# Sparse attention in a three-layer kernel: compression weights in long rows, requested at the last group's products, and one bias table of 256 columns a head

## What is computed

```python
def compress(kv, pos, w1, w2):
    idx = jnp.arange(n_cmp)[:, None] * CMP_STRIDE + jnp.arange(CMP_BLOCK)[None, :]   # 15 blocks of 32, stride 16
    blocks = kv[:, idx] + pos[None, None, :, None, :]
    flat = blocks.transpose(0, 1, 3, 2, 4).reshape(B, n_cmp, G, CMP_BLOCK * D)
    return jax.nn.silu(flat @ w1) @ w2                                               # w1: 4096 x 128
...
    kc = compress(k_cmp, cmp_pos_k, cmp_k_w1, cmp_k_w2)
    vc = compress(v_cmp, cmp_pos_v, cmp_v_w1, cmp_v_w2)
    bias_c = table[rel_bucket(dist_c)]
    logits_c = jnp.einsum('bsghd,bigd->bghsi', qf, kc) + bias_c
    p_c = masked_softmax(logits_c, mask_c, -1)
    o_c = jnp.einsum('bghsi,bigd->bsghd', p_c, vc)
...
    o = gt[:, :, 0] * o_c + gt[:, :, 1] * o_s + gt[:, :, 2] * o_w                    # compressed, selected, window
```

## Time and profile before

| | |
|---|---|
| median of three runs | 1650.07 us (1648.35 to 1650.73) |
| profiled execution | 1647.93 us |
| its span in the trace | 1646.1 us |
| TensorE busy | 1600.4 us, 97% |
| VectorE, ScalarE, GpSimd busy | 990.7 us (60%), 792.4 us (48%), 93.1 us (6%) |
| mean granted clock of TensorE | 0.994 of full |
| DMA | 253.85 MB, mean 154 GB/s |

### The profile page before, as it was taken

The page is one execution under the profiler, slowest core; times in us unless marked ns, Lnnn a source line. Parts: engine busy times, 40 slices in busy tenths (PEclk is TensorE's granted clock), DMA queues, the critical chain, the costliest instruction groups (busy, mean ns, idle before and its releaser), DMA issues. The chain is left out here.

```text
span 1646.1 us, 32613 instructions
## 1 busy us (share of the span) xinstructions
PE 1600.4 (97%) x14261; PEld 1539.4 (94%) x14261; DVE 990.7 (60%) x1320; ACT 792.4 (48%) x1128; POOL 93.1 (6%) x83
## 2 busy tenths in 40 slices
PE   8999999999998999989999999999999999999999
PEld 7989998899997899989999899999998999999999
DVE  6686547756354664485545688887557654455643
ACT  6643226333333854454443488775455334444432
POOL 2120004000000001040000000000010000000000
PEclk9999999999998999999999999999999999999999
DMA  9543323433285337548676444444654645555572
GB/s 293 187 129 104 91 91 103 154 91 91 80 226 147 93 101 257 179 101 230 188 199 182 142 142 141 142 145 144 217 157 148 206 143 165 143 165 181 169 215 90
DMA packets 80021, 253.85 MB, mean 154 GB/s; under 512 B 9153, under 2 KB 18402, under 8 KB 79624
## 3 DMA queue, kind: packets, MB, share of 16 engines
q1 hardware_dynamic: 79224, 251.57, 50.7%
q0 software_dynamic: 656, 0.21, 0.1%
HBM read 249.06 MB, written 2.69 MB: 153 GB/s over the span
## 5 line engine op out<-in xcount | busy, mean ns | idle before, releaser
L307 DVE TENSOR_TENSOR w_lo<-w_raw,w_hi 128x1024 fp32r<-128x1024 f32 (+1 forms) x452 | 549.5, 1220 | 482.5 <-ACT w_hi L302 481.9
L302 ACT ACTIVATE w_hi<-w_raw 128x1024 fp32r<-128x1024 f32 (+1 forms) x452 | 470.5, 1045 | 575.9 <-PE ps L360 460.8
L358 PE MATMUL ps<-xt,w_hi 128*128 128x256 f32 x2224 | 652.8, 294 | 11.5 <-DVE w_lo L307 7.9
L359 PE MATMUL ps<-xt,w_hi 128*128 128x256 f32 x2224 | 632.7, 284 | 0.0
L360 PE MATMUL ps<-xt,w_lo 128*128 128x256 f32 x2224 | 632.1, 284 | 0.0
L358 PEld LDWEIGHTS ps<-xt,w_hi 128*128 128x128 f32 x2224 | 429.7, 193 | 31.0 <-issue 19.5
L359 PEld LDWEIGHTS ps<-xt,w_hi 128*128 128x128 f32 x2224 | 430.2, 193 | 1.5 <-issue 1.0
L360 PEld LDWEIGHTS ps<-xt,w_lo 128*128 128x128 f32 x2224 | 429.8, 193 | 0.0
L368 PE MATMUL ps<-w_hi,xt 128*128 128x256 f32 x576 | 169.3, 294 | 0.0
L369 PE MATMUL ps<-w_lo,xt 128*128 128x256 f32 x576 | 162.8, 283 | 0.0
L370 PE MATMUL ps<-w_hi,xt 128*128 128x256 f32 x576 | 162.8, 283 | 0.0
(11 more groups left out here) (401 smaller groups left out, 1756.8 us busy)
## 6 DMA issues: line engine op xcount, KB each, us to landing
w_raw<-in_a_w_in SPq DMA_DIRECT2D x128, 512.0 KB, 3.6
w_raw<-in_w_in SPq DMA_DIRECT2D x120, 512.0 KB, 3.6
w_raw<-in_b_w_in SPq DMA_DIRECT2D x96, 512.0 KB, 3.6
w_raw<-in_w_out SPq DMA_DIRECT2D x32, 512.0 KB, 3.6
w_raw<-in_a_w_out SPq DMA_DIRECT2D x32, 512.0 KB, 3.7
w_raw<-in_b_w_out SPq DMA_DIRECT2D x32, 512.0 KB, 3.9
arena<-in_x SPq DMA_DIRECT2D x4, 512.0 KB, 6.6
w_raw<-in_w_in SPq DMA_DIRECT2D x8, 256.0 KB, 4.3
```

Source lines behind the costliest of these rows:

```text
L302: k.nc.scalar.activation(k.wh[:, p % RING, 0:m], k.raw[:, p % RAW, 0:m], ACT.Copy).then_inc(k.hi_made, 1)
L307: k.nc.vector.tensor_tensor(k.wl[:, p % RING, 0:m], k.raw[:, p % RAW, 0:m], k.wh[:, p % RING, 0:m].bitcast(F32), ALU.subtract).then_inc(k. ...
L358: pe.matmul(os, h[:, cs], xh, start=st and ct == 0, stop=False, skip_group_check=True)
L359: pe.matmul(os, h[:, cs], xl, start=False, stop=False, skip_group_check=True)
```

## The change

`cmp_k_w1` and `cmp_v_w1` are arranged on the host into one input `cmp_w1` of 128 x 2 x 32 x 128 numbers, so that a partition's numbers lie in one row. The weights are requested in five transfers of 0.5, 1, 1, 1 and 0.5 MB. The first four (all but steps 8 to 15 of the keys' weights, whose room the recurrent mixer still uses) wait for the last products of the last group (`mm_`), with a piece behind each; then come two of the bias transfers, and after `half_done` the fifth, the second weights and the other six bias transfers.

The bias table of a head is one window of 256 columns, and the first tile reads its second half; all 8 heads stand in one room of the arena, filled by 8 transfers of 16 partitions, where 32 were. `before(h)` makes two additions (256 and 512 numbers) where one of 768 was, and `pre` counts both. The copies into `cbias` are 2 where 4 were. `NSA_WAIT` is 36 where 60 was: all stages of the sparse mixer from the second on stand 24 slots earlier (the compression at 799, the last at 963). A small scratch tile of the recurrent mixer (`small`) moves out of the arena into the room of `state`.

```diff
-NSA_A, NSA_WAIT = 5, 60
+NSA_WAIT = 36
...
+        self.bias = ar[:, 8192:8192 + NSA_H * S].rearrange("p (h n) -> p h n", h=NSA_H)
...
-    def loads(self, sp, g, done):
+    def loads(self, sp, g, products, last, done):
...
         k, a = self.k, self.a
+        w1 = a["cmp_w1"]
+        g.load(sp, products)
+        for par in range(2):
+            sp.wait_ge(last[par], 2 * sum(G_PE))
+        for i, (n, ls) in enumerate(((0, slice(0, 8)), (0, slice(16, 32)), (1, slice(0, 16)), (1, slice(16, 32)))):
+            sp.dma_start(self.w1[:, n, ls], w1[:, n, ls]).then_inc(k.w1_in, 16)
+            g.load(sp, products + 1 + i)
+        sp.wait_ge(k.rows_out, 32)
+        parts = skewed_parts(k, sp, self.bias, 0, NSA_H, self.bi)
+        for c in range(2):
+            next(parts)
         g.load(sp, done)
         sp.wait_ge(k.half_done, 2)
-        for n, nm in enumerate(("cmp_k_w1", "cmp_v_w1")):
-            sp.dma_start(self.w1[:, n], a[nm][0].rearrange("(l d) o -> d l o", d=P)).then_inc(k.w1_in, 16)
-            g.load(sp, done + 2 + 2 * n)
+        sp.dma_start(self.w1[:, 0, 8:16], w1[:, 0, 8:16]).then_inc(k.w1_in, 16)
...
-            g.load(sp, done + 5 + c // 2)
+        for c in range(2, P // SKEW):
+            next(parts)
+            g.load(sp, done + c // 2)
...
-                pe.wait_ge(self.pre, h)
+                pe.wait_ge(self.pre, 2 * h)
...
-        pe.wait_ge(k.w1_in, 32)
+        pe.wait_ge(k.w1_in, 80)
...
-            nc.vector.scalar_tensor_tensor(out=self.sc[:, h % 3], in0=k.ps[:, 0:2, 0:3 * P], scalar=scale,
-                                           in1=view(self.table(h)[:, 0:1], [[0, 2], [1, 3 * P]]),
-                                           op0=ALU.mult, op1=ALU.add).then_inc(self.pre, 1)
-            dve.wait_ge(self.pre, h + 1)
             for tt in range(NT):
                 rows = slice(P, 3 * P) if tt else slice(0, P)
+                nc.vector.scalar_tensor_tensor(out=self.sc[:, h % 3, :, rows], in0=k.ps[:, 0:2, rows], scalar=scale,
+                                               in1=view(self.bias[:, h, P - P * tt:P - P * tt + 1],
+                                                        [[0, 2], [1, P + P * tt]]),
+                                               op0=ALU.mult, op1=ALU.add).then_inc(self.pre, 1)
...
-        dve.wait_ge(self.bi, 2 * SKEW_DONE)
+        dve.wait_ge(self.bi, 16 * (P // SKEW))
...
-    small = ar[:, 4096:4352]
...
+        small = state[:].rearrange("p u i -> p (u i)")
...
-                sparse.loads(sp, g, sum(s <= at[FINISHED] for s in g.starts) + LEAD + RAW - 1)
+                products, done = (sum(s <= at[n] for s in g.starts) + LEAD + RAW - 1 for n in (FINISHED - 4, FINISHED))
+                sparse.loads(sp, g, products, mm_, done)
...
+def skewed_parts(k, e, dst, h0, heads, sem):
...
+        src = bass.AP(k.rows_dram.tensor, at, [[row - 1, SKEW], [384, heads], [1, S]])
+        e.dma_start(dst[p0:p0 + SKEW, :, :], src).then_inc(sem, 16)
+        yield
```

## The result

| | before | changed |
|---|---|---|
| median | 1650.4 us (1648.35 to 1650.76, 4 runs) | 1640.76 us (1639.38 to 1642.57, 4 runs) |
| profiled execution | 1647.93 us | 1642.57 us |
| its span | 1646.1 us | 1640.7 us |
| mean granted clock | 0.994 | 0.994 |

The ratio is 0.9947, with a 95% interval of 0.9935 to 0.996: 8.7 us less (6.6 to 10.7); the two medians are 9.6 apart. On another chip, beside some of the experiments, the changed kernel gave 1642.26 us and the ratio 0.9946 (0.993 to 0.9961). The forecast was 1644.1, a gain of 6.0 us.

A forecast was written before the change was run, and what follows sets the result against it. TensorE, busy 1600.4 of 1646.1 us, was taken as the bound; 4.7 (stall) + 1.4 (clock) - 0.15 (extra addition) = 6.0 us off the median 1650.07 gave 1644.1, range 1641.0 to 1647.0.

The forecast's parts named there:

- The first term: Head 1's scores: bias tables land in time, so VectorE's 11.4 us wait and TensorE's 4.75 go; gain 4.7 us.
- The reckoning of the bias: SyncE's queue, 484 to 508: 1.5 MB of bias and four pieces counted; 0.75 MB takes 9.6 us, all landed about 476.
- The last eighth of the weights: Requested at 462.0 after the half's end, lands in 3 to 5 us, before the compression at 475.3; no wait.
- The rate of the long rows: Weight transfers in rows of 4 and 8 KB move 416 GB/s, where short rows moved 281.
- The second term: The slow-clock stretch at 511.60 to 514.40, after TensorE's stand, should go: gain 1.4 us, or 0.
- the second stretch I keep: The half-clock stretch at 519.00 to 524.60, behind the compressed logits' products (L676), stays: gain 0.
- The price worked out for losing it: From L676's end to L604, losing the second slow stretch gains 1.6 us; TensorE then stands 2.1 us at L604.
- the first rival: No second slow stretch behind L676, being the tail of the stall's: gain 7.6 us, 1642.5 us, chance 0.24.
- The extra addition: VectorE's bias addition split in two per head: 0.15 us for the extra instruction, off the gain; bound 0 to 0.4.
- The shift: Sparse mixer steps 24 slots earlier: the earlier end wins nothing, since the products behind it did not wait.
- the evacuation ahead of head 1's addition: Rival: evacuation and split delay VectorE's addition past L676's end, costing at most 2 us: 1646.1; chance 0.15 including the clock.
- the second case: No second slow stretch behind L676: 1642.5 us, chance 0.24; less 1.5 us for spread it set the range's lower end.

The follow-up runs named there:

- late60: The changed kernel with weights (two transfers) and bias all requested after the half's end and NSA_WAIT back at 60: 1642.12 us, ratio 0.9957.
- stall60: late60 with the last of the eight bias transfers held until TensorE's first product of the second weights: 1648.03 us, ratio 0.9989.
- spread2: The changed kernel with eight more slots ahead of L605 and eight between ScalarE's Silu and head 1's exponentials: 1637.03 us, ratio 0.9931.
- wait60: The changed kernel with NSA_WAIT back at 60, all else as changed: 1641.43 us, ratio 0.9947.
- late36: The changed kernel with weights (two transfers) and bias all requested after the half's end, NSA_WAIT kept at 36: 1643.99 us, ratio 0.996.
- rows: The kernel before with only the weights rearranged into long rows, requested late, 32 bias transfers, NSA_WAIT 60: 1640.67 us, ratio 0.9944.

## Why the prediction was right, and where it fell short

The stretch from the gate to the next projection can be cut at the same rows for both pairs of profiles, in us won (the second before and the second changed one in brackets):

| part of the stretch | forecast | measured |
|---|---|---|
| first L597 to L676 (L598 to L677): the stall | 4.7 | 4.75 (5.0) |
| the same: the clock | 1.4 | 1.7 (2.2) |
| L676 to L604 (L677 to L605) | 0 | 2.0 (1.1) |
| L604 to the next waiting scores | -0.15 | -0.07 (-0.06) |
| sum | 6.0 | 8.4 (8.2) |

**The first term** held in mechanism and size. Bias landed by 478.1 at the latest, against a forecast of about 476; no wait of L845, the compression at 475.60 against 475.3, no wait over 1 us for the scores of head 1. The reckoning of the bias has a slip: from 484 to 508 the engines moved 207 GB/s, that is 5.0 MB, where the forecast counted 3.5 (bias and four pieces). At its 416 GB/s the other 1.5 MB take 3.6 us, so its 9.6 us for the last 0.75 MB of bias would have been 7.7; the slip does not explain why the bias came later than forecast. The last eighth of the weights took 5.7 us to land, not 3 to 5, with 7.7 us to spare. The first request left at 442.88 (443), and the delayed piece, issued at 443.25, stopped nobody.

**The rate of the long rows** was right while the engines were full: 424 GB/s at 446 to 448, against 416 assumed. late60, with the weights in long rows requested late, moved 422 from 464 to 475 at a share of 1.00. The prediction noted that the Trainium skill (DMA: Bandwidth & Descriptors, Specifications) asks for 512 B at least for line rate, by which the long rows would win nothing. Here the rows disagree: from 464 to 475 it was 315 GB/s at a share of 1.01 with the weights in rows of 512 B, and 375 at 0.94 when only the shape was changed, weight pieces in 4 KB rows among them both times.

**The second term** was right that the slow stretch ahead of L676 goes with the stall; stall60 brings it back with a stall of 3.15 us. The clocks of all executions, each a mean over the whole execution, bear it out: their average was 0.9939 for stall60 (10 executions) and 0.9939 for the kernel before beside it (15), and 0.9958 for spread2 (5) on the same chip; the eight sets of runs without the stall that have the kernel before beside them were all above it, by 0.0015 to 0.0037. Its size was read low. The prediction took the 2.8 us of the earlier trace rows; finer windows give 3.3, and 6.8 in the second profile, in part of which TensorE stood. The part ahead of L676 gave 1.7 and 2.2.

**The step that failed is "the second stretch I keep, since its nearest cause is L676, which is unchanged".** In the profiles of before it was 6.8 us both times; in the nine profiles of kernels without the stall at head 1's scores it was 0 once, 6.8 once, and 3.4 seven times. So it did not stay, and mostly did not go either: it halved, which gave 1.1 to 2.0 us where the sum had none. The price worked out for losing it was close: 1.6 us, and a stand of 2.1 at L604. The trace of the changed kernel gave 2.0 and 2.02. This was the first rival, at 24%, whose time of 1642.5 lies nearer the measured 1640.76 than the forecast does; the second set of runs gave 1642.26. That its term came in whole in the first profile was partly luck, as the second profile, with 1.1, shows. What halves it is not settled. That the stall does it was the theory of stall60; there the stall was back and the second stretch was 3.4 us all the same, while late60, without a stall, had 6.8. Part of it is chance from execution to execution, and one or two profiles of each kernel cannot part that from a cause. (The prediction cited the Trainium skill, TensorE: Matmul & The Clock Gate, What's actually happening, by which the number of slow products after idling differs between runs of one kernel. The two profiles of before agree: 3.3 and 6.8 us in the first stretch.)

**The extra addition** cost 0.07 against 0.15 estimated: two of them take 1.02 us where one took 0.95.

**The shift** won nothing, as forecast (wait60). That the evacuation ahead of head 1's addition would push it behind L677 did not happen either: the addition ran at 501.69 while L677 ran until 503.9.

**The range** reached down to 1641.0, and the median was 1640.76, or 1642.26 on the second chip. It was too narrow below because its lower end was the second case less 1.5 us; the clock terms of both cases had been read low together, from windows that cut the slow stretches short.

**What the prediction did not say** is that the change is more than enough. It counted the bytes of all parts towards one wait of 4.75 us, and never asked how many of them were needed: the long rows alone took out 3.8, the tables alone all of it, and the early request was needed for the shift alone, which wins nothing.

## What to carry to other kernels

When a wait at the end of a queue of transfers is removed by several edits at once, work out for each edit alone whether it already removes it: here each of two did, and a third only paid for a fourth that won nothing. A stall of TensorE can cost more than its length when half-clock time comes with it (3.15 us cost 5.2 in stall60, while 2.76 in late36 cost about its length), so look for what is left of short waits as well: 16 slots put in the right two places took out another 3.5 us of waits and made the stretch 2.4 and 3.3 us shorter, but only where they separate the releaser from what delays it. And a term for the clock, read from one execution, needs a second profile of the same kernel before it is counted, either way.

## What the runs showed of the hardware

- The same code met slow-clock stretches of different number and length: with one kernel, 10.1 us at half clock between 495 and 530 in one profile and 13.6 in another; with the changed one, none and 3.4.
- Removing the burst of 15-column products did not remove the slow stretch: one came later, at 506.0 and 508.6, around the next stand of TensorE (2.88 us). Stands of 2.76 us (late36) and 2.02 us (the changed kernel's first profile) had none behind them.
- The weights' rows set the rate: from 464 to 475, pieces of 4 KB rows among them, 315 GB/s at a DMA share of 1.01 with 512 B (before) and 375 at 0.94 with long rows (rows); with rows of 4 to 8 KB 424 at 1.03 (446 to 448, changed kernel). While six of the bias transfers were under way (462 to 476), in rows of 1 KB, each partition starting one number further left, the engines were full (share 1.07) at 205 GB/s, with the last eighth of the weights and several pieces among them.
- Single bias transfers of 128 KB took 2.8 us to land alone (stall60) and up to 10.0 in a crowd.
